# Two split units and a chain of GpSimd products moved in a two-layer hybrid transformer block

## What is computed

```python
for l in range(DEPTH):
    h = h + 0.5 * _rmsnorm(_swiglu(_rmsnorm(h, g), w_gate, w_up, w_down), g_post)      # ffn1, width 2816
    y = _token_mixing(_rmsnorm(h, g), ...)                                             # four mixers side by side
    h = h + _rmsnorm(y, mix_post_g)
    h = h + _rmsnorm(_cross_attention(_rmsnorm(h, g), _rmsnorm(mem, g), ...), xa_post_g)
    h = h + 0.5 * _rmsnorm(_swiglu(_rmsnorm(h, g), ...), g_post)                       # ffn2
```

## Time and profile before

| what | value |
|---|---|
| median of 3 runs | 1283.72 us (1281.01 to 1283.88) |
| the profiled execution's own time | 1280.59 us |
| its span | 1278.7 us |
| mean granted TensorE clock | 0.998 of full speed |
| PE, PEld busy | 1257.3 us (98%), 1069.4 us (84%) |
| DVE, ACT, POOL busy | 815.4 us (64%), 660.9 us (52%), 212.9 us (17%) |
| HBM traffic | 222.36 MB, 174 GB/s on average |

### The profile page before, as it was taken

The page is one execution under the profiler, slowest core; times in us unless marked ns, Lnnn a source line. Parts: engine busy times, 40 slices in busy tenths (PEclk is TensorE's granted clock), DMA queues, the critical chain, the costliest instruction groups (busy, mean ns, idle before and its releaser), DMA issues.

```text
span 1278.7 us, 18589 instructions
## 1 busy us (share of the span) xinstructions
PE 1257.3 (98%) x6836; PEld 1069.4 (84%) x6836; DVE 815.4 (64%) x1169; ACT 660.9 (52%) x1099; POOL 212.9 (17%) x247
## 2 busy tenths in 40 slices
PE   8999999999999999999999999999999999999998
PEld 6888888899988888888888888788998798888886
DVE  5657767785656575555676566777857566755554
ACT  6454446664445464444564544565746455544442
POOL 1715441000002010000055243400000110100000
PEclk9999999999999999999999999999999999999999
DMA  9755444424525355555455555444255243655551
GB/s 349 263 197 176 175 174 149 165 100 171 192 83 198 105 228 197 197 188 179 167 193 181 193 197 197 163 151 163 68 196 188 79 182 132 233 182 181 178 185 62
DMA packets 32442, 222.36 MB, mean 174 GB/s; under 512 B 3584, under 2 KB 4096, under 8 KB 6784
## 3 DMA queue, kind: packets, MB, share of 16 engines
q1 hardware_dynamic: 30080, 209.28, 45.8%
q10 hardware_dynamic: 2304, 12.29, 2.5%
HBM read 219.46 MB, written 2.10 MB: 173 GB/s over the span
## 4 chain that ended last, share of the span: by engine, by line
PE 94%; DVE 3%; ACT 1%; issue 1%; DMA 0%; POOL 0%; SPq 0%; POOLq 0%; ACTq 0%; DVEq 0%
PE PS L1679 89%; PE PS L1796 2%; DVE w_lo L1151 1%; PE PS L2018 1%; PE PS L1822 1%; DVE mix_out L1151 0%; DMA raw<-in_weights 0%; DVE x_lo L1154 0%; ACT work L973 0%; ACT w_hi L681 0%; PE PS L2271 0%; PE PS L2062 0%; PE PS L2002 0%; PE PS L1949 0%; ACT x_hi L729 0%
## 5 line engine op out<-in xcount | busy, mean ns | idle before, releaser
L1151 DVE TENSOR_TENSOR w_lo<-raw,w_hi 128x1024 fp32r<-128x1024 f32 (+1 forms) x378 | 477.1, 1305 | 222.9 <-ACT w_hi L681 220.0
L681 ACT ACTIVATE w_hi<-raw 128x1024 fp32r<-128x1024 f32 x368 | 369.0, 1054 | 231.3 <-PE PS L1679 227.2
L1679 PE MATMUL PS<-w_hi,x_hi 128*128 128x512 f32 (+2 forms) x1104 | 426.0, 386 | 5.0 <-DVE x_lo L1154 2.6
L1679 PE MATMUL PS<-w_lo,x_hi 128*128 128x512 f32 (+2 forms) x1104 | 414.1, 375 | 0.0
L1679 PE MATMUL PS<-w_hi,x_lo 128*128 128x512 f32 (+2 forms) x1104 | 408.5, 376 | 0.0
L1679 PEld LDWEIGHTS PS<-w_hi,x_hi 128*128 128x128 f32 x1104 | 208.7, 189 | 46.5 <-issue 5.8
L1679 PEld LDWEIGHTS PS<-w_hi,x_lo 128*128 128x128 f32 x1104 | 208.6, 189 | 38.5
L1679 PEld LDWEIGHTS PS<-w_lo,x_hi 128*128 128x128 f32 x1104 | 209.1, 189 | 34.9 <-issue 0.5
L1679 PE MATMUL PS<-w_hi,hid_hi 128*128 128x512 f32 x336 | 131.5, 391 | 0.0
L1679 PE MATMUL PS<-w_lo,hid_hi 128*128 128x512 f32 x336 | 130.8, 389 | 0.0
L742 ACT ACTIVATE work<-PS,st 128x256 f32<-128x256 f32 x88 | 42.0, 478 | 155.0 <-PE PS L1679 153.5
(11 more groups left out here) (276 smaller groups left out, 1297.4 us busy)
## 6 DMA issues: line engine op xcount, KB each, us to landing
raw<-in_weights SPq DMA_DIRECT2D x194, 1024.0 KB, 4.7
pmat<-in_mats ACTq DMA_DIRECT2D x3, 1568.0 KB, 7.7
gain<-in_post ACTq DMA_DIRECT2D x8, 512.0 KB, 3.7
zone<-mem_scratch ACTq DMA_DIRECT2D x2, 1024.0 KB, 6.1
raw<-in_weights SPq DMA_DIRECT2D x3, 512.0 KB, 7.0
h<-in_x SPq DMA_DIRECT2D x2, 512.0 KB, 6.0
zone<-in_mem SPq DMA_DIRECT2D x1, 1024.0 KB, 9.9
mem_scratch<-zone ACTq DMA_DIRECT2D x1, 1024.0 KB, 5.8
```

The source lines that it names most:

```text
L681: a.activation(w_hi[s][:, c_], raw[s][:, c_], ACT.Copy).then_inc(sem[hi_done[s]], 1)
L1151: return v.tensor_tensor(o, x_, y_, op)
L1679: return t_.matmul(o, a_, b_, start=first, stop=last)
```

## The change

Three moves, none of which adds or removes work on the data:

```diff
@@ GpSimd block @@
                 brw, biw = bc(s_b[0], 2, CH), bc(s_b[1], 2, CH)
-                pool.wait_ge(*E.at("hid_t", 9))
-                pool.sem_inc(pool_held)
                 tw = v3(proj[:, 1280:2304], "p (g j c) -> p g j c", g=PAIRS, j=CH)
                 tt(s_w[0], brw, over_c(arj, CH, 0), ALU.mult)
                 tt(tw, biw, over_c(aij, CH, 0), ALU.mult)
                 tt(s_w[0], s_w[0], tw, ALU.subtract)
-                pool.wait_ge(*E.at("hid_t", 10))
+                pool.wait_ge(*E.at("hid_t", 9))
                 pool.sem_inc(pool_held)
                 tt(s_w[1], brw, over_c(aij, CH, 0), ALU.mult)
@@ ScalarE block @@
                 a.activation(probs_t[0:NC_CMP, 0:1024], bank(6, 2)[0:NC_CMP], ACT.Copy).then_inc(sem["cmp_tc"], 1)
+                split_mid(23)
                 group_squares((1,), "cmp_done", 1)
-                split_mid(23)
@@ VectorE block @@
                     tt(s5_tiles[1][:, k], s_out[:, k], s5_tiles[0][:, k].bitcast(F32), ALU.subtract).then_inc(sem["x_split"], 1)
-                split_mid(22)
                 attention_out(1)
...
                 stt(hx, hx2, 1.0, hx, ALU.add, ALU.mult).then_inc(sem["phi_hid"], 1)
+                split_mid(22)
                 split_mid(21)
...
                 attention_out(2)
+                split_mid(23)
                 dve.wait_ge(*E.at("cmp_o", 1))
...
                 group_norm(1, 1, 2)
-                split_mid(23)
                 mixer_lo(3)
```

## The result

The changed kernel takes 1273.87 us (median of 4 runs, 1273.23 to 1274.1), the kernel before beside it 1282.37 (4 runs, 1280.89 to 1283.88). The ratio is 0.9938 (95% interval 0.9919 to 0.9956): faster by 0.6%, 8.5 us between the medians. The profiled execution of the changed kernel took 1274.1 us, its span is 1272.3 us.

The account below looks back on a forecast made before the run. TensorE's queue, 94% of the chain that ended last, was taken to bound the kernel. The terms, 3.2 + 1.5 + 0.3 = 5.0 us, taken from the median of the runs, gave 1278.8 us, range 1275.8 to 1281.4.

Parts of the forecast that it names:

- Term 1: Last chunk of ffn1: GpSimd's products a chunk sooner free VectorE's split, saving TensorE 1.61 us a layer, 3.2 in all.
- Rival (c): Last chunk of ffn1: GpSimd does not hold VectorE's split, the 4.76 us have another cause; 1281.9 us, chance 0.04.
- Term 2: Ahead of scores(2): attention_out(1) before unit 22's split ends TensorE's wait, saving 0.74 us a layer, 1.5 in all.
- term 3: Before unit 23's products: its split in VectorE's idle time lets x_lo start sooner, 0.13 us a layer, 0.26 in all.
- Rival (b): Mixers: their later waits take back the gains of Term 2 and term 3; 1280.5 us, chance 0.15.
- Rival (d): ffn1 chunks 9 and 10: collision moves onto splits b(9) and b(10), 3.5 us a layer lost; 1285.7 us, chance 0.05.
- Rival (a): TensorE's clock falls in small-matmul stretches: one fall fewer gives 1277.1 us (chance 0.16), one more 1280.5 (0.17).

Follow-up runs that it names:

- `no_wait`: Changed kernel without the wait for hid_t 9 ahead of s_w[1], so that it follows s_w[0] at once: 1274.13 us (5 runs), ratio 0.9949.
- B alone: Kernel before with only attention_out(1) put ahead of unit 22's split: 1277.19 us (8 runs), ratio 0.9968.
- the filler alone: Kernel before with three identity matmuls of 256 columns ahead of TensorE's wait in front of scores(2): 1279.76 us (12 runs), ratio 0.9991.
- A alone: Kernel before with only GpSimd's products moved a chunk sooner: 1275.56 us (6 runs), ratio 0.9958.
- without B twice: Changed kernel with unit 22's split back ahead of attention_out(1), measured two times: medians 1275.23 and 1275.80 us (12 runs), ratios 0.9966 and 0.9947.
- `pool_copy`: Kernel before with GpSimd's last addition for s_w[1] replaced by a copy of one tensor: 1277.17 us (10 runs), ratio 0.9965.
- C alone: Kernel before with only unit 23's split moved into idle time: 1281.22 us (12 runs), ratio 1.0002.

## Why the forecast missed

**Term 1, right.** 1.61 forecast, 1.62 found. The model behind it, that a VectorE instruction with two SBUF inputs and a GpSimd instruction take turns, gave four ends (three of GpSimd's, one of VectorE's) within 0.1 us once the later start is taken off. Advanced Engine Details and Errata, in the Trainium skill, section VectorE Performance Modes, names two-port Vector instructions alone as blocked by GpSimd; if no others were, the split would have stayed as it was. The rows disagree, 4.76 and 2.36 us. GPSIMD Engine Reference, of the Trainium skill too, names in section Key points also Vector instructions with two SBUF inputs, and with that the rows agree. Rival (c) is out.

**Term 2 and term 3, right.** 0.78 and 0.14 us a layer against 0.74 and 0.13. Rival (b) is out: TensorE kept its lead to the end of both mixers. Rival (d) is out: the collision moved onto b(9) and b(10) as feared, and even the heavier one of `no_wait` cost nothing.

**The failed step** is "I take 5.0 from the median: 1278.8 us". It treats the 3.1 us between the median and the profiled execution as something that the changed kernel has as well. The runs show two things in its place. The median of the first three runs, 1283.72, was on the high side; over 54 more it is 1281.3, and that is 2.4 of the 4.9 us by which the forecast was too high. It is the luck of a small sample. The rest is mostly falls of the clock, which the changed kernel seldom has. The first three runs have no clock on record, but of the 54 every one above 1282.2 us had 0.995 or less. The profiled execution itself held one fall of some 1.5 us. An execution of the changed kernel like the profiled one but without a fall is 1280.6 - 5.1 - 1.5 + 0.25 = 1274.2, and 1274.1 was measured. The sum had ended at 1275.6 before the median was brought in, which is 1.7 us off and the fall that it kept.

**Rival (a) was the right mechanism with too little in it.** It was priced at one fall fewer, 1277.1 us, with a chance of 0.16, and one more fall was held to be as likely. Found: 29 of 54 executions of before are lowered, and 2 of 16 of the changed kernel (16 of 54 against 2 of 16 with the line at 0.996). Against the 1281.3 of the 54 runs the changed kernel is 7.3 us faster: 5.1 from TensorE's queue, as forecast, and 2.2 that are left for the clock. The trace gave a reason against equal chances: the change takes waits out, one of them ahead of a stretch where the fall had been seen, and puts none in. That is an argument from afterwards; that this wait decides it, no run shows.

**What stays open.** B alone and the filler alone make falls rare (1 lowered execution of 20), both ahead of the stretch where the fall was. But the runs without the transposes' wait and with that of B also have fewer (A alone, without B twice, `pool_copy`: 6 of 28), though the transposes' wait ends 98 us or more ahead of any fall seen under the mixers. Its loss shifts all that follows by 1.6 us; whether that shift is the reason, or the chip was kinder in those runs, no run here tells. So it is shown, by the profiled executions, that time beyond the queue is lost in falls; what makes them rarer in the changed kernel is not. Nor was tried whether filler in the other place, some 60 us ahead of `scores(2)`, would remove the last falls.

## What to carry to other kernels

Before a forecast is taken off a median, ask what the median holds that the profiled execution does not: here the mean granted clock beside each time says it, 0.994 or 0.995 standing 2 to 5 us above the middle of those at 0.998. Take the median from more than three runs when the gain forecast is of the size of their spread. A wait of TensorE ahead of a stretch in which the clock has been seen to fall may be worth more than its length; price that as a rival, and test it, since here the same wait was worth 3.9 us alone and 1.2 to 1.9 on top of the other terms. And work of GpSimd on large SBUF tensors is moved not to where GpSimd is free but to where VectorE's split has the slack for its turns; those can be worked out instruction by instruction beforehand.

## What the hardware showed beyond that

- The granted clock fell to its lower level (1.2 of 2.4 GHz) in stretches in which TensorE had no idle time at all in the profile, 7.00 of 7.00 us in C alone. What it did before that fall was 24 products with 65 columns and eight with one. Before the falls behind `scores(2)` it made transposes and 16 products with 15 columns, and then up to six of full size before the clock fell.
- Three useless matmuls of 0.46 us each, put into a wait of 0.74 us, made a kernel 0.1% faster in the median (interval 0.9979 to 1.0003, so perhaps not at all) where 0.1% slower was due; 1 of 12 executions was lowered, against 14 of 25 beside it.
- A GpSimd copy, with a single input, holds VectorE's split too, by 1.0 us for 128x1024, against 2.4 for an operation on two full tensors.
